# Expert slots filled and emptied by indexed transfers instead of one-hot products, with the last stage in the experts' block

## The reference

```python
logits = (h @ router_w) + router_b              # 320 x 8
top_v, top_i = lax.top_k(logits, 2)
wts = softmax(top_v)
gate = sum(one_hot(top_i, 8) * wts[..., None])  # two nonzero weights per token
for e in range(8):
    y = y + gate[:, e:e+1] * ((silu(h @ w_gate[e]) * (h @ w_up[e])) @ w_down[e])
x = x + gt_f * rmsnorm(y, post_ffn_g)           # last stage, output y
```

## Time and profile before

| | us |
|---|---|
| median of 3 runs | 1821.39 (1816.81 to 1824.66) |
| profiled execution | 1820.95 |
| its span, first to last instruction | 1819.2 |
| TensorE busy | 1640.1 (90%) |
| VectorE busy | 1151.9 (63%) |
| ScalarE busy | 972.5 (53%) |
| POOL busy | 49.2 (3%) |
| mean granted TensorE clock | 0.944 |

### The profile page before, as it was taken

The page is one execution under the profiler, slowest core; times in us unless marked ns, Lnnn a source line. Parts: engine busy times, 40 slices in busy tenths (PEclk is TensorE's granted clock), DMA queues, the critical chain, the costliest instruction groups (busy, mean ns, idle before and its releaser), DMA issues. The chain is left out here.

```text
span 1819.2 us, 26540 instructions
## 1 busy us (share of the span) xinstructions
PE 1640.1 (90%) x10764; PEld 1395.4 (77%) x10764; DVE 1151.9 (63%) x1222; ACT 972.5 (53%) x1147; POOL 49.2 (3%) x148
## 2 busy tenths in 40 slices
PE   6998889856999996987775999999999999999995
PEld 4997456655999995985565888888888888888884
DVE  3881431145444334345735788889897989889895
ACT  2542422256333335233644777767776777677774
POOL 2320100000000000000000000000000000000000
PEclk8998899878999997998986999999999999999998
DMA  9715669472554434222020899999999999999991
GB/s 328 219 47 189 234 228 383 146 202 70 159 143 128 150 116 140 94 93 105 7 87 21 305 366 364 348 320 354 362 359 313 351 363 353 342 331 361 359 352 69
DMA packets 260573, 421.23 MB, mean 232 GB/s; under 512 B 12166, under 2 KB 125007, under 8 KB 260431
## 3 DMA queue, kind: packets, MB, share of 16 engines
q1 hardware_dynamic: 258656, 415.74, 66.6%
q10 hardware_dynamic: 1788, 3.70, 0.6%
HBM read 414.34 MB, written 5.07 MB: 231 GB/s over the span
## 5 line engine op out<-in xcount | busy, mean ns | idle before, releaser
L2560 DVE TENSOR_TENSOR w_lo_late<-raw,w_hi_late 128x2048 fp32r<-128x2048 f32 x264 | 600.6, 2288 | 93.7 <-ACT w_hi_late L2492 92.2
L2492 ACT ACTIVATE w_hi_late<-raw 128x2048 fp32r<-128x2048 f32 x264 | 505.3, 1918 | 172.9 <-PE bank L353 172.9
L351 PE MATMUL bank<-w_hi_late,hg_hi 128*128 128x512 f32 (+1 forms) x768 | 290.6, 378 | 1.0 <-DVE w_lo_late L2560 0.5
L353 PE MATMUL bank<-w_hi_late,hg_lo 128*128 128x512 f32 (+1 forms) x768 | 286.3, 373 | 0.0
L352 PE MATMUL bank<-w_lo_late,hg_hi 128*128 128x512 f32 (+1 forms) x768 | 286.0, 372 | 0.0
L272 DVE TENSOR_TENSOR w_lo_main<-raw,w_hi_main 128x2048 fp32r<-128x2048 f32 (+1 forms) x50 | 112.3, 2249 | 119.4 <-ACT w_hi_main L265 119.4
L351 PEld LDWEIGHTS bank<-w_hi_late,hg_hi 128*128 128x128 f32 x768 | 144.9, 189 | 31.5 <-DVE w_lo_late L2560 7.2
L353 PEld LDWEIGHTS bank<-w_hi_late,hg_lo 128*128 128x128 f32 x768 | 144.8, 189 | 25.6
L352 PEld LDWEIGHTS bank<-w_lo_late,hg_hi 128*128 128x128 f32 x768 | 145.0, 189 | 24.0
L351 PE MATMUL bank<-w_hi_late,act_hi 128*128 128x512 f32 x352 | 138.5, 393 | 0.0
L353 PE MATMUL bank<-w_hi_late,act_lo 128*128 128x512 f32 x352 | 137.3, 390 | 0.0
(11 more groups left out here) (463 smaller groups left out, 2887.9 us busy)
## 6 DMA issues: line engine op xcount, KB each, us to landing
raw<-in_moe_w_gate SPq DMA_DIRECT2D x88, 1024.0 KB, 6.9
raw<-in_moe_w_up SPq DMA_DIRECT2D x88, 1024.0 KB, 7.2
raw<-in_moe_w_down SPq DMA_DIRECT2D x88, 1024.0 KB, 7.3
ada_delta<-in_ada_w SPq DMA_DIRECT2D x40, 1024.0 KB, 8.4
raw<-in_gdn_w_in SPq DMA_DIRECT2D x16, 1024.0 KB, 7.9
raw<-in_ffn_w_gate SPq DMA_DIRECT2D x22, 512.0 KB, 4.0
raw<-in_ffn_w_up SPq DMA_DIRECT2D x22, 512.0 KB, 5.2
ada_start<-in_ada_w SPq DMA_DIRECT2D x8, 1024.0 KB, 16.6
```

Source lines behind the costliest of these rows:

```text
L351: pe.matmul(out, w_hi, x_hi, start=start, stop=False)
L353: return pe.matmul(out, w_lo, x_hi, start=False, stop=stop)
L2492: act.activation(k.w_hi[:, m % SPL, :], k.raw[:, m % RAW, :], ACT.Copy).then_inc(k.hi_ready, 1)
L2560: dve.tensor_tensor(k.w_lo[:, m % SPL, :], k.raw[:, m % RAW, :], k.w_hi[:, m % SPL, :], ALU.subtract).then_inc(k.raw_split, 1)
```

## The change

Tokens go to slots and back through a table in HBM, `slot_rows_far`, with 8 x 384 = 3072 rows of 1024 float32 (384 slots for each expert). A token's two rows in it are `SLOTS * expert + rank`.
- In attention POOL clears a row and SP writes it over the whole table (12.6 MB); SP waits for that before it leaves the block.
- In the router block the ranks become row numbers (`row`), and POOL issues six indirect transfers that store each token tile at its first and at its second row. The tokens are kept as float32 (`h_tok`); high and low parts of them, `slot`, the gate products and `put` and `pick` are gone.
- In the experts' block POOL fetches each expert's 128 rows two experts ahead, with an index per partition (`idx`), TensorE transposes them (8 transposes of 128 x 128), and ScalarE and VectorE write the high and low parts. The expert's output goes unscaled to SBUF, half by each of the two engines, and POOL stores it over the expert's rows. The clear of `y_tok` is gone.
- After the last expert POOL fetches each token tile's two rows (six transfers) into `y_tok` and `h_tok`. The last stage is now code in the same block (`Final`): ScalarE scales the first row by its weight, VectorE adds the second times its own, tile by tile, and the rest is as before. Coefficient products (L2480) stay where they were.
- Small POOL additions (`hold`) with a semaphore of their own stand before each fetch and store.

```diff
@@ attention_phase
         def _(sp):
             sp.dma_start(v_past[:], ...).then_inc(caches_in, 16)
+            sp.wait_ge(zeroed, 1)
+            sp.dma_start(slots.rearrange("(n p) d -> p n d", p=P),
+                         zero[:].unsqueeze(1).to_broadcast([P, NE * SLOTS // P, D])).then_inc(cleared_in, 16)
             sp.wait_ge(k.stores[0], k.n_store[0])
+            sp.wait_ge(cleared_in, 16)
+        @block.gpsimd
+        def _(pool):
+            pool.memset(zero[:], 0.0).then_inc(zeroed, 1)
@@ router_phase
+            pool.wait_ge(rows_ready, 1)
+            pool.wait_ge(tok_kept, 6)
+            for t, (t0, nt) in enumerate(TOKEN_TILES):
+                for c in range(2):
+                    pool.indirect_dma_start(slots[:, :], bass.IndirectOffsetOnAxis(ap=row[0:nt, t, c:c + 1], axis=0), h_tok[0:nt, t, :],
+                                            None).then_inc(scattered_in, 16)
             for n in range(6):
-                pe.wait_ge(tok_lo, n + 1)
+                pe.wait_ge(tok_kept, n + 1)
                 turn(k.xT, n).then_inc(x_turned, 1)
+            dve.tensor_tensor(one[:], one[:], place[:], ALU.mult)
+            run(dve.tensor_tensor(two[:], two[:], place[:], ALU.mult))
+            dve.tensor_reduce(row_f[:, :, 0:1], one[:], AX.X, ALU.add)
+            run(dve.tensor_reduce(row_f[:, :, 1:2], two[:], AX.X, ALU.add))
+            dve.tensor_copy(row[:], row_f[:]).then_inc(rows_ready, 1)
-            for n in range(6):
-                low(n)
@@ expert_phase, POOL
-            pool.memset(k.y_flat[:], 0.0).then_inc(added, 1)
+            pool.wait_ge(scattered_in, 96)
+            def fetch(e):
+                pool.indirect_dma_start(xg[:, e % 2, :], None, slots[:, :], bass.IndirectOffsetOnAxis(ap=idx[:, e:e + 1], axis=0)).then_inc(
+                    x_in[e % 2], 16)
+            def run_round(r):
+                pool.wait_ge(idx_ready, r + 1)
+                hold(0)
+                fetch(0)
+                fetch(1)
+                for e in range(NE):
+                    if e + 2 < NE:
+                        pool.wait_ge(x_turned, r * (2 * NE) + (2 * e + 2))
+                        hold(1 + e)
+                        fetch(e + 2)
+                    pool.wait_ge(out_low, r * NE + (e + 1))
+                    pool.wait_ge(out_high, r * NE + (e + 1))
+                    hold(NE + e)
+                    pool.indirect_dma_start(slots[:, :], bass.IndirectOffsetOnAxis(ap=idx[:, e:e + 1], axis=0), out[:, e % 2, :],
+                                            None).then_inc(out_sent[e % 2], 16)
+                for b in range(2):
+                    pool.wait_ge(out_sent[b], sent(r, NE))
+                hold(2 * NE)
+                for t, (t0, nt) in enumerate(TOKEN_TILES):
+                    for c, dst in enumerate((k.y_tok, h_tok)):
+                        pool.indirect_dma_start(dst[0:nt, t, :], None, slots[:, :],
+                                                bass.IndirectOffsetOnAxis(ap=row[0:nt, t, c:c + 1], axis=0)).then_inc(y_in[t], 16)
@@ expert_phase, TensorE
+            def turn_x(r, e, half):
+                if half == 0:
+                    pe.wait_ge(x_in[e % 2], r * (NE // 2 * 16) + (e // 2 * 16 + 16))
+                for q in range(4):
+                    last = pe.transpose(Y[half][:, q * P:(q + 1) * P], xg[:, e % 2, (4 * half + q) * P:(4 * half + q + 1) * P], k.ident[:])
+                last.then_inc(x_turned, 1)
-                for s in range(STEPS):
-                    gather(r, 0, s, k.ps[s], k.ps[STEPS + s])
-                put_back(r, 0)
+                for half in range(2):
+                    turn_x(r, 0, half)
-                        if e and j in (2, 6, 10, 14, 18, 21):
-                            scatter(r, e - 1, (j + 2) // 4 if j == 21 else j // 4)
-                            ... (gather and put_back in the down slabs)
+                        if e < NE - 1 and d in (2, 4):
+                            turn_x(r, e + 1, d // 2 - 1)
-                for u in range(UNITS):
-                    scatter(r, NE - 1, u)
@@ expert_phase, VectorE and ScalarE
+            def keep(r, e):
+                dve.wait_ge(k.split_read, r * ROUND_SLABS + (n0 + (e + 1) * EXPERT_SLABS))
+                if e >= 2:
+                    dve.wait_ge(out_sent[e % 2], sent(r, e))
+                dve.tensor_copy(out[:, e % 2, 512:1024], DB[1][:]).then_inc(out_high, 1)
+                if e < NE - 1 and d in (3, 5):
+                    x_low(r, e + 1, d // 2 - 1)      # x_high alike on ScalarE
@@ Final
+            act.wait_ge(self.y_in[t], n_rounds * 32)
+            act.activation(k.y_tok[0:nt, t, :], k.y_tok[0:nt, t, :], ACT.Copy, scale=self.w[0:nt, t, 0:1]).then_inc(k.sig["scaled"].sem, 1)
+            dve.scalar_tensor_tensor(k.y_tok[0:nt, t, :], self.h_tok[0:nt, t, :], self.w[0:nt, t, 1:2], k.y_tok[0:nt, t, :], ALU.mult,
+                                     ALU.add).then_inc(k.sig["added"].sem, 1)
```

More of the change, by code:

```diff
@@ L2164, with router_phase @@
 ROUNDS = (T + P - 1) // P
[L2165 to L2170, removed]
+SLOTS = ROUNDS * P
+def router_phase(k, h32, h_tok, row, w, idx_f, idx, rounds, slots, scattered_in):
     nc = k.nc
@@ L2289, in _, with expert_phase @@
             dve.scalar_tensor_tensor(rounds[:], most[:, 0:1], float(2 * P), most[:, 1:2], ALU.is_gt, ALU.add)
+            run(dve.memset(place[:], 0.0))
             for ts, nt in both:
-                last = dve.scalar_tensor_tensor(slot[0:nt, ts, :], rp[0:nt, ts, :], 1.0, picked[0:nt, ts, :], ALU.add, ALU.mult)
+                last = dve.tensor_tensor(place[0:nt, ts, :], rp[0:nt, ts, :],
+                                         base8[0:nt].unsqueeze(1).to_broadcast([nt, ts.stop - ts.start, NE]), ALU.add)
             run(last)
[L2293 to L2298, removed]
-            for n in range(6):
-                low(n)
+            dve.tensor_tensor(one[:], one[:], place[:], ALU.mult)
[3 more added lines that the diff above has]
+            dve.tensor_copy(row[:], row_f[:]).then_inc(rows_ready, 1)
 def turn_after(c):
     return 4 * (c + 1) + 1 if c < CH - 1 else UP_SLABS + 1
-def expert_phase(k, mem, h_hi, h_lo, slot, gate2, rounds):
+def expert_phase(k, mem, h_tok, row, idx_f, idx, rounds, slots, scattered_in, y_in, final, gates_ready):
     nc, i = k.nc, k.i
@@ L2321, in expert_phase @@
     gs, a32 = sb("e_silu", [P, FF_CHUNK]), sb("e_act", [P, 2, FF_CHUNK])
[L2322 to L2325, removed]
+    xg, out = sb("slot_rows", [P, 2, D]), sb("slot_out", [P, 2, D])
+    spare = sb("spare", [P, 2 * NE + 3])
     with ExitStack() as sems:
@@ L2353, in each_round, with hold @@
                     run_round(r)
[L2355 to L2361, removed]
+            return n_rounds
         @block.gpsimd
         def _(pool):
-            pool.memset(k.y_flat[:], 0.0).then_inc(added, 1)
+            pool.wait_ge(scattered_in, 96)
+            def hold(n):
+                pool.tensor_tensor(spare[:, n:n + 1], k.eps[:], k.eps[:], ALU.add).then_inc(held, 1)
+            def fetch(e):
[23 more added lines that the diff above has]
+                                                bass.IndirectOffsetOnAxis(ap=row[0:nt, t, c:c + 1], axis=0)).then_inc(y_in[t], 16)
+                for t in range(3):
+                    pool.wait_ge(y_in[t], r * 32 + 32)
+                pool.wait_ge(held, r * (2 * NE) + 2 * NE)
+            each_round(pool, run_round)
         @block.sync
@@ L2379, in _ @@
             each_round(sp, again, 1)
+            final.sp(sp)
         @block.tensor
         def _(pe):
[L2383 to L2414, removed]
+            def turn_x(r, e, half):
[4 more added lines that the diff above has]
+                last.then_inc(x_turned, 1)
@@ L2542, in run_round @@
                     split(r, g)
-                for s in range(STEPS):
-                    gather_high(r, 0, s, k.ps[s])
-                put_copy(r, 0)
+                for half in range(2):
+                    x_high(r, 0, half)
                 for g in range(ROUND_SLABS):
```

254 lines of the change are left out of this document (97 added, 157 removed).

## The result

The changed kernel takes 1810.95 us (median; 1808.53 to 1812.19), the kernel before on the same chip 1822.49: a ratio of 0.9935, interval [0.9921, 0.9949]. It is faster by 11.5 us (0.65%) where 30 were forecast, at the upper edge of the range. The profiled execution took 1811.25 us with a span of 1809.5.

What follows compares the result with a forecast made beforehand. TensorE was taken to pace the expert stage, with the feed ahead; stage products -35.7, hold-up +3, head -3.2 and tail +6 sum to -29.9 from 1820.95, giving 1791 us, range 1776 to 1812.

Steps and rivals of the forecast that it cites:

- An expert like number 2: Expert stage: an expert without gather and put-back goes from 96.2 us to 94.1, by scatter removed and transposes added.
- the head: From the turns of x to the first weight matmul: weights start 5.7 us earlier, net gain 3.2 us.
- the tail: From the last weight matmul to the end: store and six gathers lengthen 26.2 us to 32.9; 6 us lost.
- products and transposes: TensorE in the expert stage: gather, put-back and scatter products go, transposes come, 40.6 - 4.9 = 35.7 us less.
- a hold-up of 3: Expert stage: Pool's 13 transfer issues hold up VectorE and so the feed; a loss of 3 us entered.
- a gain of 4: Favourable bound of the hold-up, in us: shorter output copies end the short stalls at expert borders.
- Rival B: DMA becomes the expert stage's pace: at 370 GB/s the stage takes 771 us, the whole 1809; chance 0.14.
- loads land within 10 us: Expected in the profile after if the forecast is right; landings of 10 us and more would mean DMA paces.
- Rival C: Pool's 14 issues in a row are the price: 2.8 us each gives 1812, 3.5 gives 1822; chance 0.15.
- c: Price of one indirect transfer's issue on Pool: 1.3 us taken, between 0.37 and 4.0.
- The clear of 12.6 MB: Clearing the table in attention, within 58 us where DMA is nearly idle: costs nothing.
- The clock's 2.5 us: Start of the expert stage: some 5 us of weight matmuls run at half clock, taking back 2.5 us.

Runs made afterwards that it cites:

- e10: The changed kernel with an unused pad of 160 bytes ahead of the experts' tiles, run once more: 1790.02 us, ratio 0.9821 to the kernel before.
- the sweeps: The changed kernel with another place for each expert's stationary tiles, 1799.89 us, and the same with the split weights 128 bytes lower, 1802.23 us.
- e1: The changed kernel once more, unaltered: 1806.72 us, ratio 0.9911 to the kernel before.

## Why the prediction was right and wrong

**Where it failed.** The step is the stage's: "An expert like number 2 would take 96.2 - 2.8 (scatter) + 0.7 (transposes) = 94.1 us". It took each remaining weight matmul over at the old distance from start to start, 227.5 ns, and the changed kernel has 234.1. There expert 2 takes 96.0 us from its first weight matmul to expert 3's (1199.27 to 1295.29), in e10, where the old pitch holds, 93.7. The freed tiles moved the stationary operands 12,960 bytes down, by the sizes of the tiles ahead of them in the two kernels, from distance 0 to 96 modulo 256: 2976 matmuls became 6.6 ns dearer and 384 of 256 columns 2.4 cheaper. Measured whole, it is 18.2 us, 769.9 against 751.7. None of the rivals had this. By the Trainium skill ("TensorE: Matmul & The Clock Gate", Step-by-step: what each phase is for) loading the next weights takes no memory bandwidth from the running matmul, which would make the addresses of the two operands indifferent. In the sweeps they are not: the pitch moves by up to 7 ns of 227. That the load and the stream disturb each other in memory is my reading of the distance rule and not shown: no run separates it from another cause that goes by the same distance.

**The rest holds, and e10 checks it,** since it is the forecast's kernel but for the pad: 1790 where 1791 stood. That the two agree to 1 us is partly luck: the stage came out 6.2 us better than its terms, the head 2.4 and the tail 2.8 worse.
- Stage: 788.1 to 751.7, which is 36.4 less with the slow clock of the first slab in it (5.3 us in place of 2.8). Without that 38.9, where products and transposes were 35.7 and a hold-up of 3 was put on top. The hold-up didn't come: low halves take 2289 ns, as in the earlier trace rows (2288). The gain of 3.2 beyond the products is near the bound "a gain of 4". The 7.2 us of the earlier trace rows are waits of weight loads (PEld), which run under the matmul ahead of them; for the matmuls themselves the same view has

```profile
PE bank L351 <- DVE w_lo_late L2560: 0.5, 3, 0.2
```

The prediction read 7.2 as TensorE's own. Measured in the starts from 1015 us on, distances between neighbouring weight matmuls that are over 15 ns too long lose 7.6 us in sum in the kernel before and 5.5 in e10: 2.1 of the 3.2 are stalls that went. Of the rest, 0.9 is that the 42 scatter units had cost 20.6 us and not 19.7.

- Rival B, DMA: not reached. e10 moves 370 GB/s over 745 us at a DMA share of 1.01, and its loads in the stage land after 5.1 to 11.8 us (median 7.9), in the kernel before after 5.0 to 9.5 (7.2). So the sign "loads land within 10 us" was missed though rival B didn't come: no row has an engine waiting for a load, and ScalarE still waits for TensorE (141.7 us). The feed leads, with a thin margin.
- Rival C, Pool's issue: c was put at 1.3, and the scatters start (989.62 - 983.14) / 5 = 1.30 us apart. It was chosen between bounds of 0.37 and 4.0, so that it fits to the digit is luck. Beside VectorE's low half a store's issue takes 2.74 us (median); it costs nothing there, since Pool's transfers are due 70 us later. It is Pool that is held up, not VectorE.
- The clear of 12.6 MB: issued at 832.17 and landed in 39.4 us, within the attention stage; nothing lost.
- Head: 5.7 us earlier were forecast, 3.4 came. From the turns of x to the first weight matmul were 24.6 us, with 2.6 of waiting ahead; now 23.8 (23.6 in e10). The issues are as priced, and the scatters are in 3.4 us after the last (3.6). But the block ends 0.6 us after that, and 1.8 us pass between its end and fetch 0, and 4.5 in place of 3.1 between the rows' arrival and the first weight matmul; fetch 0 itself, 4.0 us for 4.9, gives 0.9 back. The clock's 2.5 us are as forecast (5.3 us for the first slab, 2.8 before).
- Tail: 6 were forecast, 8.6 measured. The last store's rows are in 5.1 us after the start of its issue (4.9 priced), but it starts at M + 1.5 and the first gather 0.8 after the rows: M + 7.5 in place of 6.0. The six issues end at M + 14.6 (14.0), and the last rows are there at M + 20.4 (17.2): gathers take 4.6 to 7.0 us from issue to landing, 5.9 in the median, and the last one 6.6 where 4.5 was priced. What follows them takes 14.5 us in place of 1.0 + 14.7: the 14.7 held a table load of ScalarE, and that now runs at 1778.44, while ScalarE waits for rows.

With the distance restored the sum is -3.3 (first weight matmul; -3.6, and a front that is 0.3 later) - 36.4 + 8.8 = -30.9, by e10's span of 1788.3 against 1819.2. The forecast's was -29.9.

## What to carry to other kernels

When tiles are freed or added, the addresses of all that come behind them change, and a TensorE-bound stage can get slower by that alone, here by 2.4% (769.9 us against 751.7). Compare the start-to-start distance of an untouched matmul before and after: where it moved with nothing waiting, try the operands' old distance before looking for a cause in what was changed. Here a pad of 160 bytes was worth more in the stage (18.2 us) than the whole change had brought (11.5, or 15.3 in e1).

## What the runs showed of the hardware

- 512-column float32r matmuls in a stream with a new 128-column stationary tile each start 227.1 to 234.1 ns apart, by the distance between stationary and moving tile modulo 256 bytes: 0 is fast, 192 nearly so (228.9 to 229.0), all others tried cost 5 to 7 ns. At granted clock 0.50 there is no difference (426.6 to 426.7 at 0, 96 and 128). With 256 columns the order is another (119.9 at 0, 113.4 at 64). No other type was tried, nor a stationary tile that stays for several matmuls.
- The issue of an indirect transfer of 128 rows on Pool takes 0.95 us and 0.30 until the next, whichever way it goes, and up to 2.82 while VectorE works on two SBUF operands; from the start of the issue to the landing are 3.6 to 7.0 us with DMA otherwise quiet, 9.1 (median of the stores) beside the loads.
- The router's block, which ends with Pool's scatters, ended 4.0 us after the last issue (3.8 in e10), 0.6 after the last landing.
